# GLA decay levels of a hybrid decoder layer: from a zero-padded query block to two row halves of TensorE

## The chip, the cores and the metric

One core of a Trainium2 chip runs one decoder layer. The metric is the time of one execution on the device, in microseconds (us); lower is better. Before the change three executions took 393.50, 393.97 and 395.26 us.

## What is computed

The layer has 256 tokens of 1024 features. One input projection feeds an ALiBi softmax attention of 8 heads and a gated linear attention (GLA) of 4 heads with key size 64 and value size 128. Both go through an output projection; then come cross attention to 256 memory tokens and a squared-ReLU MLP, each closed by a layer norm. The change touches GLA's decayed scores alone:

```python
# _gla, for each chunk of C = 64 tokens
b = jnp.cumsum(gc, axis=2)                              # gc: log of the decay, per key feature
diff = b[:, :, :, None, :] - b[:, :, None, :, :]
decay = jnp.exp(jnp.where(causal[:, :, None], diff, -jnp.inf))
attn = jnp.einsum('bhtd,bhsd,bhtsd->bhts', qc, kc, decay)
o_intra = jnp.einsum('bhts,bhse->bhte', attn, vc)
```

The decay depends on query, key and feature, so `attn` is not one matrix product. The kernel splits the causal pairs (query t, key s) by the largest block in which they part: at the level of width w, blocks of 2w tokens are cut in two, the keys lie in the first half and the queries in the second. With the decay taken relative to the border between the halves, each level is a plain product of decayed keys and decayed queries. `LEVELS = [64, 32, 16, 8, 4, 2, 1]` gives seven of them (level 0 covers pairs that lie in different chunks of one 128-token tile), and `off` does the last part, queries of the second 128 tokens against keys of the first.

## The kernel before

Each engine runs its own program in the order written in the code, and semaphores join them. Weights come in as f32 and are split into a high and a low part (`w_hi` by ScalarE, `w_lo` by VectorE, line 1106); a large product is then three products in the fast 32-bit format fp32r (lines 1702 to 1704, 1761 and 1765). The products of the levels are in full f32, and the profile shows each f32 matmul as two loads of weights and two matmuls. In this text a *pass* is one such pair.

GLA's keys and queries lie feature by token: 128 rows hold two heads of 64 features each (`r` = 0, 1), and 512 columns hold two head pairs `f` by 256 tokens (two tiles `t` of 128). For level n:

- VectorE writes exponents into `expo[n % 2]` (`exponents`, lines 1225 and 1226), and ScalarE exponentiates them (`decay`, line 792).
- GpSimd multiplies (lines 599 and 609): decayed keys into `lev[n % 2]`, all 128 rows at once; decayed queries into `lev_q[n % 2]`, head by head, 64 rows at a time. `lev_q` has room for both heads side by side (`r` is a column index too) and is zeroed beforehand, so that the other head's rows of each head's block are zero. These products count up `lev_done`, three a level.
- TensorE (`level(n)`, line 1888) does four matmuls, one for each (t, f): stationary `lev`, 128 rows by 128 key tokens; moving `lev_q`, 128 rows by 2 x 64 query columns. The zeros keep the heads apart. The result, 128 by 512, fills one bank of PSUM, `lv{n}`.
- VectorE (`masked(n)`, line 1256) copies the causal part into `att` by a predicated copy, and frees the bank.

`FRONT_FILLS` lists every use of the eight banks in order. `begin(name)` makes TensorE wait until the bank's use before is freed; `wait_full` and `wait_out` make another engine wait until a bank is filled or freed.

TensorE's order around the levels is: `two_blocks(6, 0)` (memory keys xk00, xk01), `pv0` and `pv1` (probabilities by values, on column halves: 64 stationary columns), `level(0)`, `level(1)`, `two_blocks(6, 2)` (xk10, xk11), then one of `memory_keys` or `tokens(8, 0)` between any two of levels 2 to 6; `off` (line 1899), `tokens(8, 1)`, and `av0`, `av1`, where the levels' result meets the values. `two_blocks` first does the high products of both blocks (16 matmuls, line 1761) and then the low ones (16, line 1765). `score` (lines 1858 and 1859) and `off` already work on row halves: stationary 64 rows, the two heads in alternation, each into its own bank. `diag` (line 1877) is an f32 product with only two moving columns.

Of the kernel before, what the change touches and what calls it, by code (L numbers as in the profile page):

```python
# [21 lines left out]
S = 256  # L22
# [136 lines left out]
def ff_unit(kind, n):  # L159

    if (kind, n) == ("down", 0):
# [6 lines left out]
     ("ka0", 1), ("ka1", 2), ("ka2", 3), ("ka3", 0), ("va0", 2)]  # L168
    + [(f"score{h}", b) for h, b in enumerate((4, 5, 6, 7, 1, 3, 0, 2))] + [("va1", 4)]
# [21 lines left out]
def build(nc, x, lead, memT, w_in, w_glr, w_gate_up, b_gate, gla_norm_g, w_mix_o, ln1_g, ln1_b, w_xq, w_xkv,  # L191
# [7 lines left out]
    with ctx:  # L199
# [3 lines left out]
        def sem(name):  # L203
            return ctx.enter_context(nc.semaphore(name))
# [116 lines left out]

        lev_q = [v[:, :].rearrange("p (a r s) -> p a r s", a=4, r=2) for v in (reset, qkdiag)]

# [38 lines left out]
        dve_link, act_link, pool_link = sem("dve_link"), sem("act_link"), sem("pool_link")  # L364
        zabs_done, softplus_done, cum_done = map(sem, ("zabs_done", "softplus_done", "cum_done"))
        reset_done, att_zeroed, headsel_done, half_done = map(sem, ("reset_done", "att_zeroed", "headsel_done", "half_done"))
        lev_q_zeroed = sem("lev_q_zeroed")
        bias_done, score_done, exp_done, prob_done = map(sem, ("bias_done", "score_done", "exp_done", "prob_done"))
        planes_made, probsT_made = sem("planes_made"), sem("probsT_made")
        turned_in = [sem(f"turned_in{j}") for j in range(HA // 2)]  # L370
# [39 lines left out]
        def freed(name):  # L410
            return bank_free[FILL[name][0]]
# [139 lines left out]
        def _(pool):  # L551
# [18 lines left out]
            pool.tensor_tensor(qkdiag[:], qgT, kgT, ALU.mult).then_inc(qkdiag_done, 1)  # L570
            pool.wait_ge(cum_done, 1)
            pool.memset(att[:, 0:1024], 0.0).then_inc(att_zeroed, 1)
            pool.memset(lev_q[0], 0.0).then_inc(lev_q_zeroed, 1)
            def make_planes(j):

                pool.wait_ge(prob_done, 4 * (j + 1))
# [2 lines left out]
            for j in range(HA // 2):  # L579
                make_planes(j)  # L580
            wait_full(pool, "diag")
            pool.memset(lev_q[1], 0.0).then_inc(lev_q_zeroed, 1)
            pool.wait_ge(lev_q_zeroed, 2)
            for n in range(len(LEVELS) + 1):
                w = LEVELS[n] if n < len(LEVELS) else P

                def part(v, c):
                    return v.rearrange("p (b c w) -> p b c w", c=2, w=w)[:, :, c, :]

                pool.wait_ge(decay_done, n + 1)  # L590
                if n >= 1:
                    pool.wait_ge(lev_done, 3 * n)
                if n >= 2:
                    b, before = FILL[f"lv{n - 2}"]
                    pool.wait_ge(bank_full[b], before + 1)
                if n < 2:
                    pool.wait_ge(bank_full[FILL["score7"][0]], FILL["score7"][1] + 1)

                pool.tensor_tensor(part(lev[n % 2], 0), part(kgT, 0), part(expo[n % 2], 0), ALU.mult).then_inc(lev_done, 1)
                if n == len(LEVELS):  # L600
                    pool.tensor_tensor(part(lev[n % 2], 1), part(qgT, 1), part(expo[n % 2], 1), ALU.mult)\
                        .then_inc(lev_done, 1)
                else:
                    for r in range(2):
                        own = slice(64 * r, 64 * r + 64)
                        pool.wait_ge(lev_done, 3 * n + 1 + r)
                        q, e = (v[own, :].rearrange("p (a b c w) -> p a b c w", a=4, c=2, w=w)[:, :, :, 1, :]
                                for v in (qgT, expo[n % 2]))
                        pool.tensor_tensor(lev_q[n % 2][own, :, r, :].rearrange("p a (b w) -> p a b w", w=w), q, e,
                                           ALU.mult).then_inc(lev_done, 1)  # L610
            pool.wait_ge(small_in, 32)
            for t in range(2):
                wait_out(pool, f"rg{t}")
# [481 lines left out]
        def _(dve):  # L1095
# [116 lines left out]
            def exponents(n):  # L1212


                e, c4 = expo[n % 2], cum
                if n >= 2:
                    dve.wait_ge(lev_done, 3 * (n - 1))
                else:
                    dve.wait_ge(bank_full[FILL["score7"][0]], FILL["score7"][1] + 1)
                if n < len(LEVELS) and LEVELS[n] < CHUNK:  # L1220
                    w = LEVELS[n]
                    ev = e.rearrange("p (b c w) -> p b c w", c=2, w=w)
                    cv = c4.rearrange("p (b c w) -> p b c w", c=2, w=w)
                    mid = cv[:, :, 0, w - 1:w].to_broadcast([P, 512 // (2 * w), w])
                    link(dve.tensor_tensor(ev[:, :, 0, :], mid, cv[:, :, 0, :], ALU.subtract))
                    dve.tensor_tensor(ev[:, :, 1, :], cv[:, :, 1, :], mid, ALU.subtract).then_inc(expo_done, 1)
                    return

                ev = e.rearrange("p (f c w) -> p f c w", f=2, c=4)
                cv = c4.rearrange("p (f c w) -> p f c w", f=2, c=4)  # L1230

                def last(c):
                    return cv[:, :, c, CHUNK - 1:CHUNK].to_broadcast([P, 2, CHUNK])

                if n < len(LEVELS):
                    for c in (0, 2):
                        link(dve.tensor_tensor(ev[:, :, c, :], last(c), cv[:, :, c, :], ALU.subtract))
                    link(dve.tensor_copy(ev[:, :, 1, :], cv[:, :, 1, :]))
                    dve.tensor_copy(ev[:, :, 3, :], cv[:, :, 3, :]).then_inc(expo_done, 1)
                else:  # L1240
                    link(dve.tensor_tensor(ev[:, :, 0, :], last(0), cv[:, :, 0, :], ALU.subtract))
                    link(dve.tensor_tensor(ev[:, :, 0, :], ev[:, :, 0, :], last(1), ALU.add))
                    link(dve.tensor_tensor(ev[:, :, 1, :], last(1), cv[:, :, 1, :], ALU.subtract))
                    link(dve.tensor_copy(ev[:, :, 2, :], cv[:, :, 2, :]))
                    dve.tensor_tensor(ev[:, :, 3, :], cv[:, :, 3, :], last(2), ALU.add).then_inc(expo_done, 1)

            def masked(n):
                name, w = f"lv{n}", LEVELS[n]
                b = wait_full(dve, name)
                if n == 0:  # L1250
                    dve.wait_ge(masks_in, 16)
                    dve.wait_ge(att_zeroed, 1)
                else:
                    wait_out(dve, f"lv{n - 1}")

                dve.copy_predicated(
                    att[:, 0:1024].rearrange("p (a b c w) -> p a b c w", a=8, c=2, w=w)[:, :, :, 1, :],
                    level_mask(n).rearrange("p (b c w) -> p b c w", c=2, w=w)[:, :, 1, :]
                    .unsqueeze(1).to_broadcast([P, 8, 64 // w, w]),
                    b[:, :].rearrange("p (a b w) -> p a b w", a=8, w=w)).then_inc(freed(name), 1)  # L1260

            def mix(n, name):
                b = wait_full(dve, name)
# [425 lines left out]
        def _(pe):  # L1689
# [142 lines left out]
            i.then_inc(full("z"), 1)  # L1832
            queries(1)

            def two_blocks(c, m, names, act=actA, ready=None):

                for n, name in enumerate(names):
                    b = begin(name)
                    for k in range(8):
                        if m + n == 0 and k % 4 == 0:  # L1840
                            wait_hi(unit(c, k // 4))
                            if ready is not None:
                                ready(k // 4)
                        high(c, b, k, m + n, act)
                for n, name in enumerate(names):
                    for k in range(8):
                        if m + n == 0 and k % 4 == 0:
                            wait_lo(pe, unit(c, k // 4))
                        i = low(c, bank[FILL[name][0]], k, m + n, act)
                    i.then_inc(full(name), 1)  # L1850
# [30 lines left out]
            def level(n):  # L1881


                pe.wait_ge(lev_done, 3 * n + 3)
                b = begin(f"lv{n}")
                for a in range(4):
                    t, f = divmod(a, 2)
                    i = pe.matmul(b[:, a * P:(a + 1) * P], lev[n % 2][:, f * S + t * P:f * S + (t + 1) * P],  # L1888
                                  lev_q[n % 2][:, 2 * f + t, :, :], start=True, stop=True)
                i.then_inc(full(f"lv{n}"), 1)  # L1890

            wait_lo(pe, MEM_UNIT)
            def off():
                pe.wait_ge(lev_done, 3 * len(LEVELS) + 2)
                banks = [begin("off0"), begin("off1")]
                for f in range(2):
                    for r in range(2):
# [31 lines left out]
                                  probsT[:, h * 384 + S:h * 384 + 384], start=False, stop=True)  # L1929
                i.then_inc(full(f"pv{n}"), 1)  # L1930
            level(0)
            level(1)
            two_blocks(6, 2, ["xk10", "xk11"], actB)
            memory_keys(2, 0)
            level(2)
            memory_keys(2, 1)
# [6 lines left out]
            level(6)  # L1943
            off()
            tokens(8, 1, B, "xv01")
            for name in ("vg0", "vg1", "off0", "off1", "lv6"):
                wait_out(pe, name)
            for t in range(2):
                b = begin(f"av{t}")
# [244 lines left out]
```

## Time and profile before

| | |
|---|---|
| median of three runs | 393.97 us (393.50 to 395.26) |
| the profiled execution | 393.74 us, of which the span from first to last instruction is 391.8 us |
| TensorE matmul (PE) busy | 386.1 us, 99% |
| TensorE weight load (PEld) busy | 328.8 us, 84% |
| VectorE (DVE) / ScalarE (ACT) / GpSimd (POOL) busy | 350.1 / 266.9 / 89.6 us |
| chain of work that ended last | PE 96%, DVE 2%, DMA 1% |
| granted clock of TensorE | full over the whole span |

PE and PEld are one engine, seen as the matmuls and as the loads of weights, which mostly run under the matmul before. The durations of rows overlap, since matmuls are pipelined: what one of them costs is read from the distance between starts, not from its duration. A merged row such as "0.98 ... x8" covers eight records from the first start to the last end.

### The profile page before, as it was taken

How to read it: one execution, taken by the hardware profiler on the slowest of the kernel's cores; microseconds unless marked ns; L12 is line 12 of the kernel's file. 1: busy time of each engine (PE TensorE's matmuls, PEld its weight loads, DVE VectorE, ACT ScalarE, POOL GpSimd, SP SyncE). 2: the span in 40 equal slices, each digit the busy share in tenths (PEclk: the TensorE clock that was granted, in tenths of full speed). 3: DMA queues.
4: the chain of work that ended last, by engine and by line, in shares of the span. 5: the costliest groups of instructions: out<-in, count | busy, mean ns of one | idle time of the engine just before them, and what ended most of it. 6: DMA issues, size and time to landing. Idle time of an engine off the chain costs nothing.

```text
span 391.8 us, 5609 instructions
## 1 busy us (share of the span) xinstructions
PE 386.1 (99%) x2068; PEld 328.8 (84%) x2068; DVE 350.1 (89%) x450; ACT 266.9 (68%) x345; POOL 89.6 (23%) x83
## 2 busy tenths in 40 slices
PE   9999999999999999999999999999999999999995
PEld 5888888888888888889988888888888888888883
DVE  5599599969999885969898898999999999999997
ACT  6567487986354628546773758888887877788841
POOL 2049545254950205001005300000000000000003
PEclk9999999999999999999999999999999999999999
DMA  8997739985635290664747465687777767775202
GB/s 297 372 362 256 254 106 265 264 340 186 233 120 215 66 341 25 221 208 144 207 158 270 135 232 143 216 239 239 234 224 231 228 205 234 239 234 197 50 2 107
DMA packets 31585, 81.27 MB, mean 207 GB/s; under 512 B 8038, under 2 KB 9670, under 8 KB 27462
## 3 DMA queue, kind: packets, MB, share of 16 engines
q1 hardware_dynamic: 28720, 76.39, 57.0%
q0 software_dynamic: 2160, 3.93, 5.8%
q10 hardware_dynamic: 678, 0.59, 0.5%
q8 instruction: 17, 0.28, 0.3%
q14 instruction: 10, 0.08, 0.1%
HBM read 78.28 MB, written 1.05 MB: 202 GB/s over the span
## 4 chain that ended last, share of the span: by engine, by line
PE 96%; DVE 2%; DMA 1%; issue 0%; ACT 0%; DVEq 0%
PE bank L1702 17%; PE bank L1703 17%; PE bank L1704 16%; PE bank L2075 13%; PE bank L1761 13%; PE bank L1765 7%; PE bank L2082 7%; PE bank L1888 2%; PE bank L1708 1%; DMA raw<-in_lead 1%; DVE X L1656 1%; PE bank L1926 0%; DVE stats L1647 0%; PE bank L1954 0%; PE bank L2003 0%; PE bank L1859 0%
## 5 line engine op out<-in xcount | busy, mean ns | idle before, releaser
L1106 DVE TENSOR_TENSOR w_lo<-raw,w_hi 128x2048 fp32r<-128x2048 f32 x30 | 71.4, 2393 | 6.8 <-ACT w_hi L679 6.8
L679 ACT CAST w_hi<-raw 128x2048 fp32r<-128x2048 f32 x32 | 60.5, 1914 | 12.7 <-PE bank L1704 11.1
L2075 PE MATMUL bank<-actA,w_hi 128*128 128x512 f32 x224 | 55.4, 390 | 0.0
L2075 PEld LDWEIGHTS bank<-actA,w_hi 128*128 128x128 f32 x224 | 42.0, 188 | 8.7
L642 POOL DMA_DIRECT2D raw<-in_w_ff x15 | 13.2, 879 | 155.7 <-DMA raw<-in_w_ff 155.7
L1702 PE MATMUL bank<-w_hi,actB 128*128 128x512 f32 x107 | 42.6, 398 | 0.0
L1703 PE MATMUL bank<-w_lo,actB 128*128 128x512 f32 x107 | 41.8, 391 | 0.0
L1704 PE MATMUL bank<-w_hi,actB 128*128 128x512 f32 x107 | 41.8, 390 | 0.0
L1761 PE MATMUL bank<-actA,w_hi 128*128 128x512 f32 x156 | 38.3, 392 | 0.0
L1702 PE MATMUL bank<-w_hi,actA 128*128 128x512 f32 x96 | 37.9, 395 | 0.0
L1704 PE MATMUL bank<-w_hi,actA 128*128 128x512 f32 x96 | 37.4, 390 | 0.0
L1703 PE MATMUL bank<-w_lo,actA 128*128 128x512 f32 x96 | 37.4, 390 | 0.0
L1761 PEld LDWEIGHTS bank<-actA,w_hi 128*128 128x128 f32 x156 | 28.4, 188 | 5.3
L2082 PEld LDWEIGHTS bank<-actA,w_lo 128*128 128x128 f32 x224 | 30.5, 190 | 2.1
L1504 DVE TENSOR_TENSOR w_lo<-raw,w_hi 128x2048 fp32r<-128x2048 f32 x14 | 32.0, 2289 | 0.1
L2082 PE MATMUL bank<-actA,w_lo 128*128 128x256 f32 x224 | 31.3, 283 | 0.0
L953 ACT CAST w_hi<-raw 128x2048 fp32r<-128x2048 f32 x15 | 28.7, 1918 | 0.0
L1704 PEld LDWEIGHTS bank<-w_hi,actB 128*128 128x128 f32 x107 | 20.1, 188 | 4.4
L1702 PEld LDWEIGHTS bank<-w_hi,actB 128*128 128x128 f32 x107 | 20.1, 188 | 4.0 <-DVE bank L1667 0.2
L1703 PEld LDWEIGHTS bank<-w_lo,actB 128*128 128x128 f32 x107 | 20.2, 188 | 3.4
L1765 PEld LDWEIGHTS bank<-actA,w_lo 128*128 128x128 f32 x160 | 21.3, 191 | 1.2
L566 POOL TENSOR_SCALAR probsT<-const 128x384 f32<-128x384 f32 x8 | 16.6, 2090 | 22.5 <-DMA const<-in_consts 22.2
(254 smaller groups left out, 887.8 us busy)
## 6 DMA issues: line engine op xcount, KB each, us to landing
raw<-in_w_ff SPq DMA_DIRECT2D x32, 1024.0 KB, 5.2
raw<-in_w_in SPq DMA_DIRECT2D x10, 1024.0 KB, 6.8
raw<-in_w_xkv SPq DMA_DIRECT2D x8, 1024.0 KB, 5.9
raw<-in_w_mix_o SPq DMA_DIRECT2D x4, 1024.0 KB, 4.9
raw<-in_w_xq SPq DMA_DIRECT2D x4, 1024.0 KB, 5.1
raw<-in_w_xo SPq DMA_DIRECT2D x4, 1024.0 KB, 5.6
raw<-in_w_ff POOLq DMA_DIRECT2D x15, 256.0 KB, 5.1
raw<-in_lead SPq DMA_DIRECT2D x6, 384.0 KB, 4.9
```

Of the source, the lines that this page charges most:

```text
L566: pool.tensor_scalar(probsT[:, h * 384:(h + 1) * 384], const[:, C_DIST:C_DIST + 384], SLOPES[h] * DA ** 0.5, None, ALU.mult).then_inc(bias ...
L679: act.copy(dst, half_view(u)).then_inc(hi_done, 1)
L953: act.copy(w_hi[:, 1, p % 2, :], half_view(u)).then_inc(up_hi, 1)
L1106: dve.tensor_tensor(dst, half_view(u), hi_part.bitcast(f32), ALU.subtract).then_inc(lo_done, 1)
L1504: dve.tensor_tensor(w_lo[:, 1, p % 2, :], half_view(ff_unit("up", p)), w_hi[:, 1, p % 2, :].bitcast(f32), ALU.subtract).then_inc(up_lo, 1)
L1702: pe.matmul(dst, stat[0], mov[0], start=start, stop=False, skip_group_check=on)
L1703: pe.matmul(dst, stat[0], mov[1], start=False, stop=False, skip_group_check=on)
L1704: return pe.matmul(dst, stat[1], mov[0], start=False, stop=stop, skip_group_check=on)
L1761: pe.matmul(dst[:, :].rearrange("p (h s) -> p h s", h=2), weight(c, k, m * P, (m + 1) * P)[0], act[:, :, k, :], start=k == 0, stop=False, ...
L1765: return pe.matmul(dst[:, S:2 * S], weight(c, k, m * P, (m + 1) * P)[1], act[:, 0, k, :], start=False, stop=k == 7, skip_group_check=True)
L2075: pe.matmul(b[:, :].rearrange("p (h s) -> p h s", h=2), hi[:, k, m * P:(m + 1) * P], actA[:, :, k, :], start=k == 0, stop=False, skip_grou ...
L2082: i = pe.matmul(b[:, S:2 * S], lo[:, k, m * P:(m + 1) * P], actA_hi[:, k, :], start=False, stop=k == 7, skip_group_check=True)
```

## The change

The queries are no longer padded: `lev_q` holds one head's queries in that head's own 64 rows, 4 x 64 columns. `level(n)` does eight matmuls instead of four, each with 64 rows stationary (128 key tokens) and 64 query columns moving; head 0 works on the upper row half of the array and writes bank `lv{n}`, head 1 on the lower and writes `lw{n}`. GpSimd's two query products become one on 128 rows, the zeroing of `lev_q` goes, and `lev_done` counts two a level. VectorE's predicated copy becomes two, each of half the size. The banks are dealt out anew, and `level(1)` moves from before `two_blocks(6, 2)` to between its high and its low products.

```diff
-    + [("lv0", 4), ("lv1", 5), ("xk10", 2), ("xk11", 0), ("xk20", 1), ("lv2", 6), ("xk21", 2), ("lv3", 7),
-       ("xk30", 0), ("lv4", 4), ("xk31", 1), ("lv5", 5),
-       ("xv00", 0), ("lv6", 6), ("off0", 7), ("off1", 4), ("xv01", 1), ("av0", 5), ("av1", 6)]
+    + [("lv0", 4), ("lw0", 5), ("xk10", 2), ("xk11", 0), ("lv1", 6), ("lw1", 7), ("xk20", 1), ("lv2", 4), ("lw2", 5),
+       ("xk21", 2), ("lv3", 6), ("lw3", 7), ("xk30", 0), ("lv4", 4), ("lw4", 5), ("xk31", 1), ("lv5", 6), ("lw5", 7),
+       ("xv00", 0), ("lv6", 4), ("lw6", 5), ("off0", 7), ("off1", 6), ("xv01", 1), ("av0", 5), ("av1", 6)]
...
-        lev_q = [v[:, :].rearrange("p (a r s) -> p a r s", a=4, r=2) for v in (reset, qkdiag)]
+        lev_q = [v[:, 0:256].rearrange("p (a s) -> p a s", a=4) for v in (reset, qkdiag)]
...
-            pool.memset(lev_q[0], 0.0).then_inc(lev_q_zeroed, 1)
...
-            pool.memset(lev_q[1], 0.0).then_inc(lev_q_zeroed, 1)
-            pool.wait_ge(lev_q_zeroed, 2)
...
-                    pool.wait_ge(lev_done, 3 * n)
+                    pool.wait_ge(lev_done, 2 * n)
                 if n >= 2:
-                    b, before = FILL[f"lv{n - 2}"]
-                    pool.wait_ge(bank_full[b], before + 1)
+                    wait_full(pool, f"lv{n - 2}")
+                    wait_full(pool, f"lw{n - 2}")
...
-                    for r in range(2):
-                        own = slice(64 * r, 64 * r + 64)
-                        pool.wait_ge(lev_done, 3 * n + 1 + r)
-                        q, e = (v[own, :].rearrange("p (a b c w) -> p a b c w", a=4, c=2, w=w)[:, :, :, 1, :]
-                                for v in (qgT, expo[n % 2]))
-                        pool.tensor_tensor(lev_q[n % 2][own, :, r, :].rearrange("p a (b w) -> p a b w", w=w), q, e,
-                                           ALU.mult).then_inc(lev_done, 1)
+                    q, e = (v.rearrange("p (a b c w) -> p a b c w", a=4, c=2, w=w)[:, :, :, 1, :] for v in (qgT, expo[n % 2]))
+                    pool.tensor_tensor(lev_q[n % 2].rearrange("p a (b w) -> p a b w", w=w), q, e, ALU.mult)\
+                        .then_inc(lev_done, 1)
...
-                dve.copy_predicated(
-                    att[:, 0:1024].rearrange("p (a b c w) -> p a b c w", a=8, c=2, w=w)[:, :, :, 1, :],
-                    level_mask(n).rearrange("p (b c w) -> p b c w", c=2, w=w)[:, :, 1, :]
-                    .unsqueeze(1).to_broadcast([P, 8, 64 // w, w]),
-                    b[:, :].rearrange("p (a b w) -> p a b w", a=8, w=w)).then_inc(freed(name), 1)
+                w = LEVELS[n]
+                for r, name in enumerate((f"lv{n}", f"lw{n}")):
+                    b = wait_full(dve, name)
...
+                    dve.copy_predicated(
+                        att[:, 0:1024].rearrange("p (a r b c w) -> p r a b c w", a=4, r=2, c=2, w=w)[:, r, :, :, 1, :],
+                        level_mask(n).rearrange("p (b c w) -> p b c w", c=2, w=w)[:, :, 1, :]
+                        .unsqueeze(1).to_broadcast([P, 4, 64 // w, w]),
+                        b[:, 0:256].rearrange("p (a b w) -> p a b w", a=4, w=w)).then_inc(freed(name), 1)
...
             def level(n):
-                pe.wait_ge(lev_done, 3 * n + 3)
-                b = begin(f"lv{n}")
+                pe.wait_ge(lev_done, 2 * n + 2)
+                names = (f"lv{n}", f"lw{n}")
+                banks = [begin(name) for name in names]
                 for a in range(4):
                     t, f = divmod(a, 2)
-                    i = pe.matmul(b[:, a * P:(a + 1) * P], lev[n % 2][:, f * S + t * P:f * S + (t + 1) * P],
-                                  lev_q[n % 2][:, 2 * f + t, :, :], start=True, stop=True)
-                i.then_inc(full(f"lv{n}"), 1)
+                    for r in range(2):
+                        own = slice(64 * r, 64 * r + 64)
+                        i = pe.matmul(banks[r][:, a * 64:(a + 1) * 64], lev[n % 2][own, f * S + t * P:f * S + (t + 1) * P],
+                                      lev_q[n % 2][own, 2 * f + t, :], start=True, stop=True)
+                        if a == 3:
+                            i.then_inc(full(names[r]), 1)
...
             level(0)
-            level(1)
-            two_blocks(6, 2, ["xk10", "xk11"], actB)
+            two_blocks(6, 2, ["xk10", "xk11"], actB, between=lambda: level(1))
```

## Rows read from the trace of the kernel before

**Rows 1.** The page: busy time of each engine; shares of the last chain.
```profile
PE 386.1 (99%) x2068; PEld 328.8 (84%) x2068; DVE 350.1 (89%) x450; ACT 266.9 (68%) x345; POOL 89.6 (23%) x83
PE 96%; DVE 2%; DMA 1%; issue 0%; ACT 0%; DVEq 0%
```

**Rows 2.** Waits of PE: waiting for whom, us, times, longest (two largest, PE; POOL's, PEld).
```profile
PE bank L2161 <- issue: 1.5, 1, 1.5
PE bank L1753 <- PEq L2187: 0.8, 1, 0.8
...
PEld bank L1888 <- POOL qkdiag L609: 0.2, 1, 0.2
```

**Rows 3.** Timeline, levels 0, 1 and 3: start, us, engine, line, merged count.
```profile
86.49 0.97 PEld L1888 LDWEIGHTS bank<-reset,qk 128*128 128x128 f32 x8 [0.17 <-POOL qkdiag L609]
87.38 0.97 PEld L1888 LDWEIGHTS bank<-qkdiag,qk 128*128 128x128 f32 x8
88.27 3.52 PEld L1761 LDWEIGHTS bank<-actB,w_hi 128*128 128x128 f32 x16
...
100.34 0.98 PEld L1888 LDWEIGHTS bank<-qkdiag,qk 128*128 128x128 f32 x8
...
101.24 1.69 PEld L1761 LDWEIGHTS bank<-actB,w_hi 128*128 128x128 f32 x8
```

**Rows 4.** Timeline of diag: f32, 128 stationary columns, two moving columns.
```profile
71.44 1.08 PEld L1877 LDWEIGHTS bank<-headsel,qkdiag 128*128 128x128 f32 x8
71.67 0.95 PE L1877 MATMUL bank<-headsel,qkdiag 128*128 128x2 f32 x8
72.45 0.19 PEld L1702 LDWEIGHTS bank<-w_hi,actA 128*128 128x128 f32 x1
72.48 0.49 PE L1702 MATMUL bank<-w_hi,actA 128*128 128x512 f32 x1
```

**Rows 5.** Timeline, narrow windows: from level 6 into off and out again.
```profile
115.00 0.28 PE L1888 MATMUL bank<-reset,qk 128*128 128x128 f32 x1
...
115.20 0.19 PEld L1899 LDWEIGHTS bank<-qk 64*128 64x128 f32 x2
115.20 0.38 PE L1899 MATMUL bank<-qk 64*128 64x128 f32 x2
...
115.31 0.30 PEld L1899 LDWEIGHTS bank<-qk 64*128 64x128 f32 x4
...
115.53 0.19 PEld L1899 LDWEIGHTS bank<-qk 64*128 64x128 f32 x2
...
115.85 0.19 PEld L1702 LDWEIGHTS bank<-w_hi,actB 128*128 128x128 f32 x1
115.85 0.50 PE L1702 MATMUL bank<-w_hi,actB 128*128 128x512 f32 x1
```

**Rows 6.** One line's instructions: duration in ns min/median/max, off's matmuls.
```profile
L1899 PE MATMUL bank<-qk x8: 272/272/373, 115.2 to 115.6; 64*128 64x128 f32 x8
```

**Rows 7.** Timeline: into the scores, from a matmul of 512 columns.
```profile
46.53 0.39 PE L1704 MATMUL bank<-w_hi,actA 128*128 128x512 f32 x1
46.85 0.50 PE L1858 MATMUL bank<-qk 64*128 64x128 f32 x4
```

**Rows 8.** Timeline, other engines around the levels.
```profile
88.68 1.29 DVE L1268 TENSOR_TENSOR actA<-bank,actA 128x512 fp32r<-128x512 f32 x2
...
104.52 1.92 POOL L609 TENSOR_TENSOR qkdiag<-gla,qk 64x256 f32<-64x256 f32 x2
...
105.64 0.73 DVE L1256 COPY_PREDICATED att<-const,bank 128x512 f32<-128x512 int32 x1
...
107.72 0.98 PEld L1888 LDWEIGHTS bank<-qkdiag,qk 128*128 128x128 f32 x8
```

More of the change, by code:

```diff
@@ L366, in build @@
         reset_done, att_zeroed, headsel_done, half_done = map(sem, ("reset_done", "att_zeroed", "headsel_done", "half_done"))
-        lev_q_zeroed = sem("lev_q_zeroed")
         bias_done, score_done, exp_done, prob_done = map(sem, ("bias_done", "score_done", "exp_done", "prob_done"))
@@ L1216, in exponents @@
                 if n >= 2:
-                    dve.wait_ge(lev_done, 3 * (n - 1))
+                    dve.wait_ge(lev_done, 2 * (n - 1))
                 else:
@@ L1247, in masked @@
             def masked(n):
[L1248 to L1254, printed above, removed]
-                dve.copy_predicated(
-                    att[:, 0:1024].rearrange("p (a b c w) -> p a b c w", a=8, c=2, w=w)[:, :, :, 1, :],
-                    level_mask(n).rearrange("p (b c w) -> p b c w", c=2, w=w)[:, :, 1, :]
-                    .unsqueeze(1).to_broadcast([P, 8, 64 // w, w]),
-                    b[:, :].rearrange("p (a b w) -> p a b w", a=8, w=w)).then_inc(freed(name), 1)
+                w = LEVELS[n]
+                for r, name in enumerate((f"lv{n}", f"lw{n}")):
+                    b = wait_full(dve, name)
+                    if n == 0:
+                        dve.wait_ge(masks_in, 16)
+                        dve.wait_ge(att_zeroed, 1)
+                    else:
+                        wait_out(dve, f"lv{n - 1}" if r == 0 else f"lw{n - 1}")
+                    dve.copy_predicated(
[3 more added lines that the diff above has]
+                        b[:, 0:256].rearrange("p (a b w) -> p a b w", a=4, w=w)).then_inc(freed(name), 1)
             def mix(n, name):
@@ L1833, in _, with two_blocks @@
             queries(1)
-            def two_blocks(c, m, names, act=actA, ready=None):
+            def two_blocks(c, m, names, act=actA, ready=None, between=None):
                 for n, name in enumerate(names):
@@ L1844, in two_blocks @@
                         high(c, b, k, m + n, act)
+                if between is not None:
+                    between()
                 for n, name in enumerate(names):
@@ L1881, in level @@
             def level(n):
-                pe.wait_ge(lev_done, 3 * n + 3)
-                b = begin(f"lv{n}")
+                pe.wait_ge(lev_done, 2 * n + 2)
+                names = (f"lv{n}", f"lw{n}")
+                banks = [begin(name) for name in names]
                 for a in range(4):
                     t, f = divmod(a, 2)
-                    i = pe.matmul(b[:, a * P:(a + 1) * P], lev[n % 2][:, f * S + t * P:f * S + (t + 1) * P],
-                                  lev_q[n % 2][:, 2 * f + t, :, :], start=True, stop=True)
-                i.then_inc(full(f"lv{n}"), 1)
+                    for r in range(2):
[4 more added lines that the diff above has]
+                            i.then_inc(full(names[r]), 1)
             wait_lo(pe, MEM_UNIT)
             def off():
-                pe.wait_ge(lev_done, 3 * len(LEVELS) + 2)
+                pe.wait_ge(lev_done, 2 * len(LEVELS) + 2)
                 banks = [begin("off0"), begin("off1")]
@@ L1945, in _ @@
             tokens(8, 1, B, "xv01")
-            for name in ("vg0", "vg1", "off0", "off1", "lv6"):
+            for name in ("vg0", "vg1", "off0", "off1", "lv6", "lw6"):
                 wait_out(pe, name)
```

## Prediction

> **What bounds the kernel now.** I read the page first. TensorE's matmuls are busy for 386.1 of 391.8 us, and the chain of work that ended last is 96% PE [rows 1]. VectorE is busy for 350.1 us, close behind, so it has to be asked of every edit whether it makes VectorE late. The table of waits comes next: PE's two largest waits are 1.5 us at the very end of the program and 0.8 us in the warm-up, and the only wait on GpSimd's level products is 0.2 us [rows 2]. So TensorE's own occupation by each instruction sets the time: what a level costs on it more or less goes nearly one for one into the end, and what GpSimd saves is worth nothing. The timeline of the levels says what a level costs. Level 0's loads start at 86.49, level 1's at 87.38, and the next work's at 88.27: 0.89 us for 8 passes, 0.111 us each; level 3 takes from 100.34 to 101.24, 0.90 us, and the work around it follows without a gap [rows 3]. All seven levels together are 7 x 0.89 = 6.2 us, the most that any edit of them could save.
>
> **Part by part: the passes.** Before, a level is 4 matmuls of 2 passes each; each pass loads 128 columns of weights and streams 128 columns. After, it is 8 matmuls, 16 passes, in two halves of the array: 8 passes on each half, each loading 128 columns and streaming 64. Two questions decide: do the halves run side by side, and does a pass with 64 columns take less time than one with 128?
>
> To the first, `off` answers. It is written as the new level is (64 rows stationary, heads in alternation, one bank each). Its loads start in pairs: two at 115.20, the next from 115.31, the last two at 115.53. Eight passes thus take four slots of 0.11 us [rows 5]. The halves do run side by side.
>
> To the second, `diag` answers, as far as the whole array goes. It has the same stationary shape and only 2 moving columns, and still its eight passes run from 71.67 to the next matmul at 72.48, 0.81 us, or 0.10 a pass; from start to start of the loads, 71.44 to 72.45, with the first waiting out the matmul before it, it is 1.01 us for eight [rows 4]. Between 2 and 128 moving columns there is nearly no difference (0.10 against 0.111), so the load of 128 stationary columns sets the pass, and the change keeps 128 of them. I take 0.11 us a slot, 8 slots, 0.88 us: the saving against 0.89 is 0.01 to 0.02 us a level. The bounds: 0.11 if the load sets the slot; 0.055 if the stream does, half of `off`'s, with half its columns.
>
> The Trainium skill has a rule on each side here. TensorEngine Tiling (Array Packing), section "Theoretical Speedup", promises up to 2x for a dimension of at most 64, and both the contraction and the moving side are 64 here. TensorE: Matmul & The Clock Gate, section "LDWEIGHTS (loading the stationary operand)", says that a load's time goes by its columns and that its rows don't matter; the two moving columns of diag side with it.
>
> **Part by part: going into and out of row halves.** The last full pass before `off` starts at 115.00, and the usual distance would put the next at 115.11. But `off`'s first loads start only at 115.20, and its first matmuls are recorded at the same time with 0.38 us where the usual is 0.27 [rows 5, 6], so the load isn't hidden and the first pass starts in effect at 115.31: 0.20 us lost. On the way out, the last pass of `off` starts at 115.64 (four slots from 115.20 and the exposed load); the next would follow at 115.75, but the load of L1702 starts at 115.85 and is exposed too, so that its matmul (0.50 us against the usual 0.39) starts in effect at 115.96: 0.21 us lost [rows 5]. A round trip thus costs 0.41 us, and full levels pay nothing of the kind, since they have the array shape of the work around them [rows 3]. On the way in after a 512-column matmul, 46.53 to 46.85 is 0.32 us, longer than the 0.20 after 128 columns by about the longer stream [rows 7, 5]; so the gap is the stream plus some 0.09 us, and the way out of a level with only 64 columns should be 0.05 us cheaper than out of `off`. I take 0.36 us a round trip, with bounds of 0.33 and 0.41.
>
> How many are there? Levels 1 to 5 each stand between full-array work: five round trips, 5 x 0.36 = 1.8 us. Level 1 is among them because the move puts it alone between the high and low products of `two_blocks(6, 2)`. Level 0 comes after `pv1`, which is on column halves, and its loads wait already (86.49, after the 0.20 us gap that pv1 leaves); it adds the way out alone, 0.15 us. Level 6 is followed by `off`, which pays for both ways today: the way in moves ahead of level 6, and nothing is added. Sum: 1.8 + 0.15 - 7 x 0.015 (slots) = 1.85 us, between 1.6 and 2.1 with the bounds.
>
> **Part by part: the rest.** GpSimd's two query products (1.92 us for level 5, 104.52 to 106.44) become one of some 0.9; TensorE took up that level at 107.72 [rows 8], 1.3 us later, so this gives nothing, nor do the memsets, which run before the first level. VectorE does 14 predicated copies instead of 7. One of 128 x 512 takes 0.73 [rows 8]; two halves take between 0.73 (no fixed part) and 1.46 (all fixed), and the start of TensorE's later work must hold for that. The tightest place is the bank of level 5: the copy of level 3 ends at 106.37 and TensorE wants the bank at 107.72, so there is 1.35 us of cover, to which TensorE's own delay by then (four levels, some 1.3 us) is added; four levels of copies can take at most 4 x 0.73 = 2.9 us of these 2.65, and by any likely price (0.2 us a level) 0.8. I take nothing. `level(1)` in its new place needs banks 6 and 7, which `mix` on VectorE frees at 89.97 [rows 8]; TensorE gets there after 16 high products, at about 91.3 (level 0 to 87.6, then 3.7 us). Nothing waits. Behind the levels VectorE gets its inputs from TensorE, and both move together.
>
> **The sum.** The profiled execution took 393.74 us (391.8 of span, 1.9 around it), 0.23 below the median of the runs. The forecast is 393.74 + 1.85 = 395.6 for it, and 393.97 + 1.85 = 395.8 as a median: slower by 0.47%.
>
> **The rivals.**
> - *The stream sets the slot (faster).* If two halves can load faster than the whole array does, or the load of one half hides under the other's work, a slot falls to as little as 0.055 us. That saves 7 x 8 x 0.055 = 3.1 us, and with the 1.85 it is 1.25 us less: 392.7. It turns into a gain from a slot of 0.11 - 1.85 / 56 = 0.077 us down. For it: `off` streams 128 columns, so its 0.11 doesn't separate load from stream on halves. Against it: diag [rows 4]. This is what the "Theoretical Speedup" rule of the skill's page on tiling amounts to. Chance 0.06.
> - *Load and stream of one half don't overlap.* Then a slot is 0.11 + 0.055, which adds 56 x 0.055 = 3.1 us: 398.9. Against it: `off` would have slots of 0.22, and has 0.11. The skill says, in TensorE: Matmul & The Clock Gate, "The mechanism", that a load runs under a matmul only with other row groups; the trace disagrees. Chance 0.04.
> - *The halves don't run side by side*, that is, the change doesn't do what it says: 16 passes in a row, 7 x 8 x 0.11 = 6.2 us more: 402. `off` and its pairs speak against it. Chance 0.03.
> - *A bank comes free late.* The doubled copies on VectorE delay TensorE by some 0.2 us at each of three or four levels, or later where the `w_lo` parts are due: 0.5 to 1.0 us on top, 396.3 to 396.8. Against it: the cover of 1.35 us and more. Chance 0.07.
>
> **How the numbers follow.** The forecast has 0.80. Its own spread (1.6 to 2.1 us, and 0.3 us or more of the median itself, as the three runs lie 1.8 us apart) lies on both sides of 0.5%, which is 1.97 us and about what a measurement of this kernel can tell from no change. I give 0.50 of it to within 0.5% and 0.30 to slower. The two dear rivals and the late bank give 0.12 to slower and 0.02 to within; the fast rival (392.7 is -0.3%) gives 0.02 to within and 0.04 to faster, for slots lower yet. Faster 0.04, within 0.54, slower 0.42. The range is 394.5 to 397.0: the bounds of the sum, the late bank, and the spread of the median; it leaves out the fast rival and the two dear ones.
>
> **What would show it.** In the trace after, a level's loads come in pairs 0.11 us apart, eight pairs. The first load starts 0.2 to 0.3 us after the last full matmul, and the next full one's load 0.15 us after the level's last start, both with a first matmul that is recorded 0.1 us too long. From the last full matmul to the first exposed one it is 1.2 us more than without the level. PE's waits on banks or on `lev_done` stay at nothing, and the stretches behind `av1` have the same lengths. Slots well below 0.11, or halves that take turns, would make the forecast wrong.

## The result, and the profile after

The changed kernel takes 395.70 us (median; 395.13 to 397.63) where the kernel before takes 393.59: a ratio of 1.0056, 95% interval 1.0047 to 1.0065. It is slower by 2.1 us, inside the forecast range of 394.5 to 397.0 and 0.1 us from the forecast 395.8; that it lies so near is in part luck, as the account below says. A second comparison gave 1.0050 (1.0038 to 1.0063).

The page of the changed kernel, busy time and last chain (line numbers are those of the changed kernel; `level`'s matmul, L1888 before, is L1887):

```profile
span 393.8 us, 5732 instructions
PE 387.9 (99%) x2124; PEld 329.3 (84%) x2124; DVE 348.6 (89%) x457; ACT 266.7 (68%) x345; POOL 81.5 (21%) x74
PE 96%; DVE 2%; DMA 1%; issue 0%; ACT 0%; DVEq 0%
```

TensorE stays the bound, with the same shares as in [rows 1]. The span is 2.0 us longer and GpSimd 8 us less busy, which bought nothing.

The timeline of the loads of levels 0 to 4 and 6, of `off`, and of what stands behind `off` (start, length, line, merged count):

```profile
86.46 0.97 PEld L1887 LDWEIGHTS bank<-reset,qk 64*128 64x128 f32 x16 [0.17 <-issue]
91.35 0.97 PEld L1887 LDWEIGHTS bank<-qkdiag,qk 64*128 64x128 f32 x16 [0.35 <-POOL reset L602]
97.27 0.97 PEld L1887 LDWEIGHTS bank<-reset,qk 64*128 64x128 f32 x16
101.30 0.97 PEld L1887 LDWEIGHTS bank<-qkdiag,qk 64*128 64x128 f32 x16
105.33 0.97 PEld L1887 LDWEIGHTS bank<-reset,qk 64*128 64x128 f32 x16
...
116.06 0.97 PEld L1887 LDWEIGHTS bank<-reset,qk 64*128 64x128 f32 x16 [0.35 <-issue]
116.94 0.53 PEld L1899 LDWEIGHTS bank<-qk 64*128 64x128 f32 x8
117.59 0.19 PEld L1696 LDWEIGHTS bank<-w_hi,actB 128*128 128x128 f32 x1
```

Two readings carry the rest of the text. The *period* is the distance from one level to the next with the same memory keys between them: 4.03 us here (101.30 to 105.33), and 7.38 us for two before, 3.69 us each (levels 3 and 5, 100.34 and 107.72 [rows 3, 8]). So a level costs 0.34 us more. The *stretch* is the distance from level 0's first load to the first load behind `off`: 117.59 - 86.46 = 31.13 us, against 115.85 - 86.49 = 29.36 before [rows 3, 5]: 1.77 us more.

Inside level 3, by narrow windows of the timeline: the last pass before, the first pair, the last pair, and the way out:

```profile
101.09 0.28 PE L1759 MATMUL bank<-actB,w_lo 128*128 128x256 f32 x1
...
101.30 0.19 PEld L1887 LDWEIGHTS bank<-qkdiag,qk 64*128 64x128 f32 x2
101.30 0.33 PE L1887 MATMUL bank<-qkdiag,qk 64*128 64x64 f32 x2
...
102.13 0.28 PE L1887 MATMUL bank<-qkdiag,qk 64*128 64x64 f32 x2
102.34 0.50 PE L1755 MATMUL bank<-actB,w_hi 128*128 128x512 f32 x1
```

Both halves work at once (two loads at 101.30, two matmuls at 102.13). Seven slots lie between the first and the last pair, the first with an exposed load; 0.97 us for sixteen loads is the length that eight had before [rows 3]. In front of the level there are 0.21 us between starts where 0.11 is usual, behind it 0.21 again, and the first full matmul is recorded with 0.50 instead of 0.39, its load not hidden.

### The profile page after: what moved, and what is told of

Its sections match the earlier page's. It is cut to its first block, busy times and chain, and to the rows that moved or that the text cites. A ratio compares the mean times of both kernels' runs of the same rounds, so it can differ in the third digit from the quotient of the medians.

```text
span 393.8 us, 5732 instructions
## 1 busy us (share of the span) xinstructions
PE 387.9 (99%) x2124; PEld 329.3 (84%) x2124; DVE 348.6 (89%) x457; ACT 266.7 (68%) x345; POOL 81.5 (21%) x74
## 4 chain that ended last, share of the span: by engine, by line
PE 96%; DVE 2%; DMA 1%; issue 0%; ACT 0%; DVEq 0%
PE bank L1696 17%; PE bank L1697 16%; PE bank L1698 16%; PE bank L1755 13%; PE bank L2074 13%; PE bank L1759 7%; PE bank L2081 7%; PE bank L1887 2%; PE bank L1702 1%; DMA raw<-in_lead 1%; DVE X L1650 1%; PE bank L1926 0%; DVE stats L1641 0%; PE bank L1953 0%; PE bank L2002 0%; PE bank L1855 0%
## 5 line engine op out<-in xcount | busy, mean ns | idle before, releaser
L2081 PE MATMUL bank<-actA,w_lo 128*128 128x256 f32 x224 | 31.3, 283 | 0.0
L1759 PE MATMUL bank<-actA,w_lo 128*128 128x256 f32 x160 | 21.7, 283 | 0.0
```

The costliest lines, as they stand in the source:

```text
L1759: return pe.matmul(dst[:, S:2 * S], weight(c, k, m * P, (m + 1) * P)[1], act[:, 0, k, :], start=False, stop=k == 7, skip_group_check=True)
L2081: i = pe.matmul(b[:, S:2 * S], lo[:, k, m * P:(m + 1) * P], actA_hi[:, k, :], start=False, stop=k == 7, skip_group_check=True)
```

## The experiments

As in the prediction, a *slot* is the time from one pass to the next (in halves or quarters, from one group of passes that start together to the next). In this section a *passage* is one change of TensorE from the full array to another array shape and back. The theory is that a passage costs 0.34 us and that a slot is as long as the longer of its load and its stream. The rivals are lateness on VectorE or GpSimd, and a slot set by something else.

**Fewer passages.** Level 1 back behind level 0, in the other column half of the same banks:

```diff
-                banks = [begin(name) for name in names]
+                second = n == 1
+                banks = [bank[FILL[name][0]] if second else begin(name) for name in names]
+                at = 256 if second else 0
...
-            two_blocks(6, 2, ["xk10", "xk11"], actB, between=lambda: level(1))
+            level(1)
+            two_blocks(6, 2, ["xk10", "xk11"], actB)
```

> The changed kernel, with level 1 moved back to stand right behind level 0; to have banks for it, level 1 takes the other column half of level 0's two banks, and VectorE's copies of level 0 wait for level 1 too. The arithmetic is the same. Theory (each passage of TensorE from full-array work to row halves and back costs it about 0.34 us): one passage fewer, 0.34 us less than the changed kernel, so a ratio to the kernel before of 1.0047 where the changed kernel has 1.0056. Rival (the extra time comes from VectorE's and GpSimd's side, copies and banks that are late): no gain, or a loss, since the copies wait longer.

Measured: ratio 1.0042 (1.0029 to 1.0055). The stretch settles what the time alone can't, since the intervals overlap. Loads of level 0, level 1, and behind `off`:

```profile
86.61 0.97 PEld L1893 LDWEIGHTS bank<-reset,qk 64*128 64x128 f32 x16 [0.17 <-issue]
87.50 0.98 PEld L1893 LDWEIGHTS bank<-qkdiag,qk 64*128 64x128 f32 x16
...
117.42 0.19 PEld L1700 LDWEIGHTS bank<-w_hi,actB 128*128 128x128 f32 x1
```

30.81 us, 0.32 less than in the changed kernel. Level 1 follows level 0 after 0.89 us, exactly as on the full array [rows 3]: without a passage the row halves cost neither more nor less than before.

The same for levels 2 with 3 and 4 with 5 (`n in (1, 3, 5)`, and `level(2)`, `level(4)` moved down one block):

> As the run before, and also levels 2 and 3 back to back, and 4 and 5, each pair in the two column halves of one pair of banks; level 2 waits for level 3's place and level 4 for level 5's. Four groups of levels are left on row halves: 0 with 1, 2 with 3, 4 with 5, and 6 with off. Theory (passages): three passages fewer than the changed kernel, 3 x 0.34 = 1.0 us less; ratio to the kernel before about 1.003. Rival (VectorE and GpSimd late): GpSimd's products for levels 4 to 7 wait 3 us longer for TensorE, so the time should rise.

Measured: 1.0023 (1.0013 to 1.0033). Its loads start at 85.96 (level 0) and, behind `off`, at

```profile
116.09 0.19 PEld L1701 LDWEIGHTS bank<-w_hi,actB 128*128 128x128 f32 x1
```

That is 30.13 us, 1.00 less than the changed kernel for three passages, 0.33 each. The rival's longer wait of GpSimd happened ahead of level 4's keys (4.9 us by its timeline, 2.1 in the changed kernel) and cost nothing.

**What sets the slot.** The change cut into 64 stationary key tokens, on quarters of the array:

```diff
                     t, f = divmod(a, 2)
-                    for r in range(2):
-                        own = slice(64 * r, 64 * r + 64)
-                        i = pe.matmul(banks[r][:, a * 64:(a + 1) * 64], lev[n % 2][own, f * S + t * P:f * S + (t + 1) * P],
-                                      lev_q[n % 2][own, 2 * f + t, :], start=True, stop=True)
...
+                    for c in range(2):
+                        for r in range(2):
+                            own = slice(64 * r, 64 * r + 64)
+                            k0 = f * S + t * P + 64 * c
+                            i = pe.matmul(banks[r][64 * c:64 * c + 64, a * 64:(a + 1) * 64], lev[n % 2][own, k0:k0 + 64],
+                                          lev_q[n % 2][own, 2 * f + t, :], start=True, stop=True)
...
```

> The changed kernel with each matmul of a level cut into two of 64 stationary key tokens, so that the four quarters of the array work (two row halves by two column halves): 16 matmuls a level, each with 64 stationary and 64 moving columns. The arithmetic is the same. Theory (the load of the stationary columns sets the slot of 0.11 us): slots of 0.055 us, 8 a level, 0.44 us a level instead of 0.88, 7 x 0.44 = 3.1 us less than the changed kernel; ratio to before about 0.998. Rival (the slot is a floor for passing instructions or for one pass whatever its size): the slots stay at 0.11 or, with twice the instructions, double; 0 to 6 us more.

Measured: 0.9975 (0.9966 to 0.9984), faster than the kernel before. Loads of levels 2 and 3, the matmuls of level 3 and behind it, and the loads of level 6 and `off`:

```profile
96.56 0.56 PEld L1889 LDWEIGHTS bank<-reset,qk 64*64 64x64 f32 x32
...
100.17 0.56 PEld L1889 LDWEIGHTS bank<-qkdiag,qk 64*64 64x64 f32 x32
100.17 0.69 PE L1889 MATMUL bank<-qkdiag,qk 64*64 64x64 f32 x32
...
100.80 0.73 PE L1755 MATMUL bank<-actB,w_hi 128*128 128x512 f32 x2
...
113.69 0.56 PEld L1889 LDWEIGHTS bank<-reset,qk 64*64 64x64 f32 x32 [0.35 <-issue]
114.31 0.52 PEld L1901 LDWEIGHTS bank<-qk 64*128 64x128 f32 x8
```

Thirty-two loads take 0.56 us where sixteen took 0.97. A level with its way out lasts 0.63 us (100.17 to 100.80) instead of 1.04 (101.30 to 102.34), and the period is 3.61 us, 0.42 less than in the changed kernel and 0.08 less than before. With 64 moving columns in both kernels, only the stationary columns of a pass differ: the load set the slot. The whole stretch (86.57 to 114.96) is 28.39 us, 2.74 less than in the changed kernel, where the theory had 3.1. Some of what is missing is at level 6, which is 0.62 us ahead of `off` (113.69 to 114.31) where it was 0.88 (116.06 to 116.94), a saving of 0.26 and not 0.42: from quarters to the row halves of `off` the array changes its shape once more.

Quarters and pairs together:

> Levels in pairs and on quarters, both of the edits above. If both theories hold the gains add: 3.1 + 1.0 = 4.1 us less than the changed kernel, which is 2 us less than the kernel before, ratio 0.995. If only the passages hold, it is 1.0 us less than the run on quarters alone.

Measured: 391.66 us, ratio 0.9952 (0.9940 to 0.9965), 2 us faster than the kernel before. Loads of level 0, level 2 with 3, and behind `off`:

```profile
85.89 0.56 PEld L1896 LDWEIGHTS bank<-reset,qk 64*64 64x64 f32 x32 [0.17 <-issue]
...
98.32 0.56 PEld L1896 LDWEIGHTS bank<-reset,qk 64*64 64x64 f32 x32
98.78 0.56 PEld L1896 LDWEIGHTS bank<-qkdiag,qk 64*64 64x64 f32 x32
...
113.22 0.19 PEld L1701 LDWEIGHTS bank<-w_hi,actB 128*128 128x128 f32 x1
```

The stretch is 27.33 us, 2.03 less than before. A level costs 0.46 us behind its neighbour (98.32 to 98.78) instead of 0.89. The two edits add: the stretch is 3.80 us shorter than in the changed kernel, where alone they took 1.00 and 2.74.

**The passage by itself.** One small matmul ahead of each of levels 2 to 5 in the kernel before, on 128 rows as a control (`0:128` for `0:64`) and on 64 rows, which is shown:

```diff
                 b = begin(f"lv{n}")
+                if 2 <= n <= 5:
+                    pe.matmul(b[:, 0:2], lev[n % 2][0:64, 0:P], lev[n % 2][0:64, P:P + 2], start=True, stop=True)
```

> The kernel before, with one more small matmul ahead of each of levels 2 to 5: 128 rows, 128 stationary and 2 moving columns, f32, into the level's own bank, which the level then overwrites. It is the control for the next run: the same extra instruction without a change of array shape. All theories: two passes of 0.11 us at four places, 0.9 us more; ratio 1.0023.

> The same as the control, but the small matmul uses the upper 64 rows alone, so that TensorE goes to row halves and back at four places, and nothing else differs. Theory (passages): on top of the control's 0.9 us, four passages of 0.38 us (0.20 on the way in, with the exposed load, and 0.20 on the way out), 1.5 us; ratio 1.006. Rival (the passage is cheap and the levels' own small passes are what costs): as the control, 1.0023.

Measured: 1.0021 (1.0012 to 1.0030) for the control, 1.0054 (1.0040 to 1.0068) on half rows. First the loads around levels 2 and 3 of the control, for the period:

```profile
96.12 0.31 PEld L1887 LDWEIGHTS bank<-qk 128*128 128x128 f32 x2
...
100.04 0.31 PEld L1887 LDWEIGHTS bank<-qk 128*128 128x128 f32 x2
```

and of the run on half rows:

```profile
97.18 0.29 PEld L1887 LDWEIGHTS bank<-qk 64*128 64x128 f32 x2
...
101.38 0.29 PEld L1887 LDWEIGHTS bank<-qk 64*128 64x128 f32 x2
101.69 0.97 PEld L1890 LDWEIGHTS bank<-qkdiag,qk 128*128 128x128 f32 x8
```

The periods are 3.92 us and 4.20 us, against 3.69 before. Two full passes cost 0.23 us; making them half-high, with nothing else changed, costs 0.28 us more. That is a passage with nearly no work in it, less than the 0.38 expected and than the 0.34 of a level. Measured by the times it is (1.0054 - 1.0021) x 393.6 / 4 = 0.32 us. The levels' own product isn't needed to lose this time.

**VectorE's part alone.** The kernel before with each copy cut in two:

```diff
-                    b[:, :].rearrange("p (a b w) -> p a b w", a=8, w=w)).then_inc(freed(name), 1)
+                for r in range(2):
+                    i = dve.copy_predicated(
...
+                        b[:, :].rearrange("p (a r s) -> p r a s", a=4, r=2)[:, r].rearrange("p a (b w) -> p a b w", w=w))
+                i.then_inc(freed(name), 1)
```

> The kernel before with VectorE's part of the change alone: each predicated copy of a level cut into two, one for each head, from the one bank. TensorE's work is as before. Theory: about 1 us more work on VectorE, all of it beside TensorE's work; ratio 1.000, within 0.1%. Rival (VectorE is late further down, where the changed kernel's trace has a wait of 0.4 us for a w_lo part in place of 0.2): 0.2 us or more on top, 1.0005 and up.

Measured: 1.0003 (0.9991 to 1.0014). The fourteen copies take 6.5 us of VectorE, where seven took 6.4. There was hardly any extra work to hide, and none of it shows in the time.

**Column halves.** All 128 rows and padded queries as before, 64 stationary columns:

```diff
-                    i = pe.matmul(b[:, a * P:(a + 1) * P], lev[n % 2][:, f * S + t * P:f * S + (t + 1) * P],
-                                  lev_q[n % 2][:, 2 * f + t, :, :], start=True, stop=True)
+                    for c in range(2):
+                        k0 = f * S + t * P + 64 * c
+                        i = pe.matmul(b[64 * c:64 * c + 64, a * P:(a + 1) * P], lev[n % 2][:, k0:k0 + 64],
+                                      lev_q[n % 2][:, 2 * f + t, :, :], start=True, stop=True)
```

> The kernel before, with padded queries and all 128 rows, but each matmul of a level cut into two of 64 stationary key tokens on column halves of the array, 128 moving columns each, into the two partition halves of the level's bank. Theory (a slot is as long as the longer of load and stream, and the passage is due for any change of the array's shape): the load falls to 0.055 us but the stream stays at 0.11, so slots stay at 0.11; level 0 follows pv1 in the same shape and levels 0 and 1 are adjacent, so their way in is saved and their way out added; levels 2 to 5 pay 0.38 each and level 6 pays 0.2 for the change from columns to rows: 1.7 us more, ratio 1.0043. Rivals: if only row halves cost a passage, 1.000; if the load alone sets the slot, 3.1 us less than that sum, 0.9965.

Measured: 1.0040 (1.0027 to 1.0052). Levels 0 and 1, 2 and 3:

```profile
86.28 0.96 PEld L1890 LDWEIGHTS bank<-reset,qk 128*64 128x64 f32 x16
87.15 0.96 PEld L1890 LDWEIGHTS bank<-qkdiag,qk 128*64 128x64 f32 x16
...
96.85 0.85 PEld L1890 LDWEIGHTS bank<-reset,qk 128*64 128x64 f32 x16
100.88 0.85 PEld L1890 LDWEIGHTS bank<-qkdiag,qk 128*64 128x64 f32 x16
```

The period is 4.03 us again: column halves cost about the same passage as row halves. Level 0, which has the shape of `pv1` here, no longer has the 0.17 us ahead of its load that it has in both kernels [rows 3]. A level behind its neighbour costs 0.87 us, though its loads are half as long: now the stream of 128 columns sets the slot. Only where load and stream both shrink, in the quarters, does the slot shrink.

**The remainder.** 1.77 of the 2.0 us of the span lie in the stretch. The rest comes at one place, 20 us later: TensorE waits 0.4 us for a `w_lo` part where it waited 0.2. The table of waits (PEld) of the changed kernel has

```profile
PEld bank L1696 <- DVE w_lo L1099: 0.4, 1, 0.4
```

and the timelines of the loads, first of the kernel before and then of the changed kernel,

```profile
137.18 0.19 PEld L1702 LDWEIGHTS bank<-w_hi,actA 128*128 128x128 f32 x1 [0.19 <-DVE w_lo L1106]
```

```profile
139.13 0.19 PEld L1696 LDWEIGHTS bank<-w_hi,actA 128*128 128x128 f32 x1 [0.39 <-DVE w_lo L1099]
```

From behind `off` to this load it is 21.54 us (117.59 to 139.13) where it was 21.33 (115.85 [rows 5] to 137.18): 0.21 us, and with the 1.77 this is the whole of the 2.0.

VectorE is late there because GpSimd's first power instruction (rms) is; the timeline of VectorE, first the kernel before, with its wait for rms:

```profile
129.34 2.19 DVE L1336 SCALAR_TENSOR_TENSOR values<-values,rms,gla 128x128 f32<-128x128 f32 x8 [0.98 <-POOL rms L626]
```

and the changed kernel:

```profile
131.29 2.19 DVE L1330 SCALAR_TENSOR_TENSOR values<-values,rms,gla 128x128 f32<-128x128 f32 x8 [1.33 <-POOL rms L619]
```

The wait is 0.35 us longer, though nothing of that step was changed. The run with passages alone (half rows, above) has 0.97, so TensorE's delay isn't the cause. Two runs side by side, the second with nine tiny writes among GpSimd's level products:

```diff
+                for k in range(2 if n in (3, 5) else 1 if n < len(LEVELS) else 0):
+                    pool.memset((reset, qkdiag)[n % 2][:, 256 + 16 * (2 * n + k):272 + 16 * (2 * n + k)], 0.0)
```

> The changed kernel unaltered, to stand beside the next run on the same chip. The passages of the levels cost 1.8 us by its trace and a later wait for a w_lo part 0.2 us; ratio to the kernel before 1.005 to 1.0056, and the wait at 0.4 us in the trace.

> The changed kernel with nine tiny GpSimd writes to unused columns among its level products, so that GpSimd again has about as many instructions ahead of its two power instructions (rms) as in the kernel before. In every kernel with GpSimd's part of the change, and in none without, the first of the two starts 0.46 us after its input instead of 0.11, which makes VectorE 0.35 us late and TensorE wait 0.4 instead of 0.2 us for a w_lo part. If the delay comes from where the instruction stands in GpSimd's program, the wait goes back to 0.2 us and the time falls by 0.2 us against the run before; if it comes from something else, both stay.

Measured: 395.76 us, 1.0050 (1.0038 to 1.0063), and with the writes 395.07 us, 1.0042 (1.0029 to 1.0054). VectorE's timeline of the second:

```profile
131.16 2.19 DVE L1332 SCALAR_TENSOR_TENSOR values<-values,rms,gla 128x128 f32<-128x128 f32 x8 [0.98 <-POOL rms L621]
```

and its waits (PEld):

```profile
PEld bank L1698 <- DVE w_lo L1101: 0.2, 1, 0.2
```

The waits are back at 0.98 and 0.2 us. The intervals of the two times overlap, so it is the trace that shows it. From behind `off` to the load that waits, first unaltered and then with the writes:

```profile
117.75 0.19 PEld L1696 LDWEIGHTS bank<-w_hi,actB 128*128 128x128 f32 x1
...
139.26 0.19 PEld L1696 LDWEIGHTS bank<-w_hi,actA 128*128 128x128 f32 x1 [0.37 <-DVE w_lo L1099]
```

```profile
117.82 0.19 PEld L1698 LDWEIGHTS bank<-w_hi,actB 128*128 128x128 f32 x1
...
139.12 0.19 PEld L1698 LDWEIGHTS bank<-w_hi,actA 128*128 128x128 f32 x1 [0.16 <-DVE w_lo L1101]
```

These are 21.51 and 21.30 us: TensorE gets its 0.21 us back. The same writes in the fastest kernel:

> The kernel with levels in pairs and on quarters, with the same nine tiny GpSimd writes. If they take the delay away, 0.2 us less than without them: ratio to the kernel before 0.9947 where it was 0.9952; otherwise 0.9952.

Measured: 391.56 us, 0.9949 (0.9936 to 0.9963), and its wait for the `w_lo` part is 0.2 us as well; the times alone don't tell 0.9947 from 0.9952. In all thirteen traces the two go together: with 83 GpSimd instructions VectorE waits 0.97 or 0.98 us for rms and TensorE 0.2 us for the `w_lo` part, with 74 it is 1.31 to 1.33 and 0.4 us.

## Why the prediction was right

**The number.** The forecast 395.8 is only 0.1 us off because two errors cancel. The kernel before has a median of 393.59 us over ten executions and not the 393.97 of three, and the change cost 2.1 us and not 1.85. So the ratio is 1.0056 and lies on the side of 0.5% that had the smaller chance (slower, 0.42), though its interval, from 1.0047, doesn't exclude the other.

**The bound.** Right: TensorE's own occupation went one for one into the end, and the 8 us that GpSimd saved were worth nothing. The 0.2 us that I read as a wait for GpSimd's products [rows 2] is none: level 0 has the same 0.17 us in the changed kernel, where GpSimd isn't named, and on column halves, the shape of `pv1`, its load starts without a gap while GpSimd's product is still at work.

**Halves side by side; the slot.** Right. Loads come in pairs, and a level behind its neighbour costs 0.89 us, as on the full array. I had expected 0.01 to 0.02 us less for each level, which didn't come. The choice of the load as what sets the slot rested on `diag`, a row of the full array [rows 4]; the quarters and the column halves now show it on divided arrays from both sides. The rule of the Trainium skill (TensorE: Matmul & The Clock Gate, "LDWEIGHTS (loading the stationary operand)") that a load's time goes by its columns and not its rows agrees: eight loads of 128 x 128 [rows 3] and eight pairs of 64 x 128 both take 0.97 us, eight groups of four of 64 x 64 take 0.56.

**The passage.** Right in mechanism and nearly in size: 0.34 us net for levels 2 to 5, where the sum had 0.36 less 0.015. Its two terms were both somewhat off and made up for each other. The way out was taken at 0.15 us lost, because only 64 columns stream; by level 3's rows the next load starts 0.21 us after the last pair, as behind `off` with 128 columns. It gets shorter only in the quarters, where the slot does. The gap goes with the slot, not with the moving columns. The way in was taken too dear, because the first pair with 64 columns makes room for the next after 0.16 us and not 0.21 (its matmul is recorded 0.33 us long, against 0.38 in `off` [rows 5]). That the passage is a cost of changing the array's shape, and not of row halves or of this product, was argued and is now shown by the small matmul (0.28 us) and by the column halves. In the Trainium skill, TensorEngine Tiling (Array Packing), "Key Properties", says that changing the tiling mode drains TensorE; the trace agrees, in that 0.21 us lie between the last start in one shape and the first in the next, where 0.11 is usual.

**How many.** Right: five whole ones, a way out for level 0, none for level 6. The stretch grew by 1.77 us where the sum had 1.85: 4 x 0.34 for levels 2 to 5, 0.32 for level 1 by the run with one passage fewer, and 0.1 for level 0, with nothing left for level 6.

**The rest at nothing.** Right for VectorE's copies and for the banks, which nobody waited for. The worst case that I gave the copies, 2.9 us against a cover of 2.65, hadn't excluded a delay; what excludes it is that cutting them in two adds 0.1 us over all seven levels. It was wrong for GpSimd: fewer instructions there were costed at zero, and in fact they made a later step start 0.35 us late, which TensorE felt as some 0.2 us. This is outside every part that I went through, since I looked only at the steps that the change moved; it also goes against my sign that the stretches behind `av1` keep their lengths. The fourth rival had the right place (a late `w_lo` part) and too high a price, with another cause.

**The rivals.** The fast one needed a slot below 0.077 us; with 128 stationary columns it stayed at 0.11. The quarters get below it, with 0.058 (0.46 us for eight), but for another reason than the rival's: the load is halved too. Slots of 0.16 or halves in turn are excluded by the same rows.

## What to carry to other kernels

A pass of a small matmul on TensorE lasts as long as the longer of its weight load (by stationary columns) and its stream (by moving columns), so dividing the array pays only if the longer of the two gets shorter; count both before dividing. Each change of the array's shape costs about a third of a microsecond here, so products on divided arrays should stand together: the same levels on row halves alone lost 2 us, and on quarters and in pairs they gained 2. In a trace, look for the first matmul of a group that is recorded 0.05 to 0.1 us longer than its neighbours and for 0.2 us ahead of its load. The table of waits doesn't name this cost as such. It has nothing for levels 2 to 5; the 0.35 us behind a matmul of 512 columns it puts down to GpSimd at 91.35 and to "issue" (no cause that the profile shows) at 116.06, though it is the same passage, and the 0.32 us between starts are the same ahead of the scores [rows 7].

## What the runs showed of the hardware that I had not expected

- The gap on the way out doesn't depend on the moving columns by themselves: from the last start it is 0.2 us with 64 and with 128 of them where 128 stationary columns are loaded, 0.2 us with 128 moving and 64 stationary ones (column halves), and 0.15 us only with 64 of each.
- Thirty-two loads and thirty-two matmuls of 64 x 64 go through TensorE in 0.69 us, from first start to last end, so its instructions are passed on fast enough for slots of 0.058 us in four quarters.
- The start of a GpSimd instruction depends on what stands ahead of it in its program: with nine instructions fewer the first power instruction made VectorE wait 1.33 us instead of 0.98, and nine idle writes, all of them 20 us or more earlier, took it back to 0.98. Whether it is the place in memory from which the instruction is fetched, or something else about the position, stays open.
